# A transformer trunk on one core: the order of VectorE, GpSimd and the load queue around two changes of stage

## What is computed

```python
h = rms_norm(x, norm1_g[l])
proj = jnp.einsum('bsd,de->bse', h, w_in[l])
...
a = pool_mixer(u, pool_w[l], pool_scale[l])
b = swa_sink_attention(q, k, v, q_norm_g[l], k_norm_g[l], sinks[l])
x = x + jnp.einsum('bse,ed->bsd', jnp.concatenate([a, b], axis=-1), w_out[l])
h2 = rms_norm(x, norm2_g[l])
hid = jnp.square(jax.nn.relu(jnp.einsum('bsd,df->bsf', h2, w_up[l])))
x = x + jnp.einsum('bsf,fd->bsd', hid, w_down[l])
```

## Time and profile before

| what | value |
|---|---|
| median of 3 runs | 909.13 us (906.57 to 909.18) |
| the profiled execution's own time | 908.38 us |
| its span, first to last recorded instruction | 906.4 us |
| share of the span: PE, DVE, ACT, POOL | 98%, 60%, 47%, 30% |

### The profile page before, as it was taken

One profiled execution on the slowest core, in us unless ns is written; L12 is line 12 of the kernel. 1 busy time (PEld: TensorE's weight loads), 2 busy tenths in 40 slices (PEclk: granted clock), 3 DMA queues, 4 the chain that ended last, 5 costly groups with the idle time before them and its releaser, 6 DMA issues.

```text
span 906.4 us, 11042 instructions
## 1 busy us (share of the span) xinstructions
PE 883.8 (98%) x4137; PEld 731.9 (81%) x4137; DVE 542.3 (60%) x817; ACT 430.1 (47%) x777; POOL 270.6 (30%) x202
## 2 busy tenths in 40 slices
...
GB/s 313 49 24 24 71 24 47 209 117 116 47 46 25 73 229 128 128 152 185 166 137 128 136 190 140 176 319 391 279 198 97 166 206 93 70 184 55 181 82 81
DMA packets 65725, 124.20 MB, mean 137 GB/s; under 512 B 3580, under 2 KB 20488, under 8 KB 65672
## 3 DMA queue, kind: packets, MB, share of 16 engines
...
...
## 4 chain that ended last, share of the span: by engine, by line
PE 88%; DVE 5%; DMA 2%; issue 2%; ACT 2%; POOL 1%; SPq 0%; DVEq 0%; ACTq 0%
PE bank L1218 27%; PE bank L1219 27%; PE bank L1220 27%; PE bank L1241 2%; PE bank L1341 1%; PE bank L1353 1%; DMA d_raw<-in_w_down 1%; DVE h_buf L1041 1%; DMA s_in<-h_keep 1%; PE bank L1329 1%; POOL mem L478 1%; PE bank L1321 1%; DVE h_buf L1031 0%; DVE wgt L910 0%; DMA mem<-in_x 0%
## 5 line engine op out<-in xcount | busy, mean ns | idle before, releaser
L1218 PE MATMUL bank<-b_op,s_op 128*128 128x512 f32 x448 | 175.1, 391 | 3.8 <-DVE b_op L1052 3.8
L1219 PE MATMUL bank<-b_op,s_op 128*128 128x512 f32 x448 | 175.0, 391 | 0.0
L1220 PE MATMUL bank<-b_op,s_op 128*128 128x512 f32 x448 | 174.9, 390 | 0.0
L538 POOL TENSOR_TENSOR b_sum<-d_raw,d_raw 128x1024 f32<-128x1024 f32 x40 | 95.8, 2396 | 207.0 <-DVE b_op L1052 207.0
L1048 DVE TENSOR_TENSOR s_op<-s_in,s_op 128x1024 fp32r<-128x1024 f32 x56 | 72.1, 1288 | 136.2 <-ACT s_op L752 136.2
L752 ACT ACTIVATE s_op<-s_in 128x1024 fp32r<-128x1024 f32 x56 | 59.4, 1060 | 182.1 <-PE bank L1220 154.3
L1009 DVE TENSOR_TENSOR ring<-raw,ring 128x512 fp32r<-128x512 f32 x96 | 93.2, 984 | 85.8 <-ACT ring L700 84.2
L1218 PE MATMUL bank<-wgt,xs 128*128 128x256 f32 (+1 forms) x320 | 123.8, 387 | 2.7 <-DVE wgt L898 2.7
L1219 PE MATMUL bank<-wgt,xs 128*128 128x256 f32 (+1 forms) x320 | 118.9, 372 | 0.0
L1220 PE MATMUL bank<-wgt,xs 128*128 128x256 f32 (+1 forms) x320 | 118.5, 370 | 0.0
L1218 PE MATMUL bank<-xs,ring 128*128 128x512 f32 x256 | 101.4, 396 | 3.9 <-issue 2.7
...
## 6 DMA issues: line engine op xcount, KB each, us to landing
...
```

The source lines that it names most:

```text
L538: nc.gpsimd.tensor_tensor(out=b_sum[G % 2], in0=group_rows(qa, g), in1=group_rows(qb, g), op=op).then_inc(b_summed, 1)
L1218: nc.tensor.matmul(out_ap, lhs[HI], rhs[HI], start=first, stop=False, skip_group_check=chained)
L1219: nc.tensor.matmul(out_ap, lhs[HI], rhs[LO], start=False, stop=False, skip_group_check=chained)
L1220: return nc.tensor.matmul(out_ap, lhs[LO], rhs[HI], start=False, stop=last, skip_group_check=chained)
```

## The change

It has five parts. The order of the same instructions changes; no arithmetic is added or removed.

1. **VectorE and GpSimd at the end of stage 1.** `normed_x1(7)` stands ahead of `w_low(2..4)`. `weight_sums` is cut in two halves. For chunk 0 they stand behind the inverse roots of tiles 5 and 6, for chunk 1 behind those of tiles 6 and 7. `w_diff` gets a second buffer, and the counter `w_sum` becomes four semaphores.
2. **Products of chunks 0 and 1.** M6, M4, M5 of chunk 0, M6 of chunk 1, M3 of chunk 0, M4, M5 of chunk 1, M1 of chunk 2, M3 of chunk 1.
3. **VectorE's order in all of stage 2.** Where the product is M4, M5 or M2, `w_low(n + 5)` stands behind `add_z`, not ahead of it. At M2 of chunk 0 it stands behind `x_combine(3)` too.
4. **SyncE in chunk 15.** `load_s(3)` and `load_s(4)` stand ahead of `keep_h(15)`, and with them the last three B11 loads behind them.
5. **`w_down` by groups.** Each block comes in 8 loads of 512 KB, where it was 4 of 1 MB, each with its own semaphore; the first three of B12 together at G = 5.

```diff
-        w_diff = place("w_diff", 184, [P, KH, P], F32)
+        w_diff = [place(f"w_diff{i}", 184 + 2 * i, [P, KH, P], F32) for i in range(2)]
...
-               + [(c, m) for c in range(2) for m in ("M6", "M4", "M5", "M3")]
-               + [(c, m) for c in range(2, NCK) for m in UP])
+               + [(0, "M6"), (0, "M4"), (0, "M5"), (1, "M6"), (0, "M3"), (1, "M4"), (1, "M5"), (2, "M1"), (1, "M3")]
+               + [(c, m) for c in range(2, NCK) for m in UP if (c, m) != (2, "M1")])
...
-            def load_d(q, quarter):
+            def load_d(q, g):
                 i, k = int(q[1]) - 1, int(q[2]) - 1
-                js = slice(4 * quarter, 4 * quarter + 4)
-                sp.dma_start(d_raw[q][:, js, :], w_down_i[i][:, js, k * BANK:(k + 1) * BANK]).then_inc(d_in[q][quarter], 16)
+                js = slice(2 * g, 2 * g + 2)
+                sp.dma_start(d_raw[q][:, js, :], w_down_i[i][:, js, k * BANK:(k + 1) * BANK]).then_inc(d_in[q][g], 16)
...
                     sp.wait_ge(up_done, done_at(c, "M6"))
-                    for quarter in range(2):
-                        load_d("B11", quarter)
+                    for g in range(2):
+                        load_d("B11", g)
                     sp.wait_ge(up_done, done_at(c, "M4"))
-                    for quarter in range(2, 4):
-                        load_d("B11", quarter)
+                    for g in range(2, 5):
+                        load_d("B11", g)
+                    load_s(3)
+                    load_s(4)
+                    for g in range(5, 8):
+                        load_d("B11", g)
...
-            for G in range(3, 7 * NG):
+            for G in range(5, 7 * NG):
                 load_s(G)
-                if 3 <= G < 7:
+                if G == 5:
+                    for g in range(3):
+                        load_d("B12", g)
+                if 6 <= G < 11:
                     load_d("B12", G - 3)
...
+            def weight_sums(c, first=True, last=True):
+
+                r = raw[c % 2]
+                w11, w12, w21, w22 = (r[:, k:k + KH, f:f + P] for f in (0, P) for k in (0, KH))
+                if first:
+                    pool.wait_ge(raw_in[c % 2], 16 * (c // 2 + 1))
+                    if c >= 2:
+                        pool.wait_ge(w_lo, done_at(c - 2, "M7"))
+                    nc.gpsimd.tensor_tensor(out=w_diff[c % 2], in0=w11, in1=w21, op=ALU.subtract).then_inc(w_diff_ready, 1)
+                    pool.wait_ge(w_diff_ready, c + 1)
+                    nc.gpsimd.tensor_tensor(out=w21, in0=w21, in1=w22, op=ALU.add).then_inc(w_one_ready, 1)
+                if last:
+                    pool.wait_ge(w_one_ready, c + 1)
+                    pool.wait_ge(w_lo, done_at(c, "M1"))
+                    nc.gpsimd.tensor_tensor(out=w11, in0=w21, in1=w11, op=ALU.subtract).then_inc(w_two_ready, 1)
+                    pool.wait_ge(w_two_ready, c + 1)
+                    pool.wait_ge(w_lo, done_at(c, "M2"))
+                    nc.gpsimd.tensor_tensor(out=w12, in0=w12, in1=w11, op=ALU.subtract).then_inc(w_four_ready, 1)
...
             for T in range(NT + 2, 2 * NT):
                 inverse_rms(T)
...
+                if T == 2 * NT - 3:
+                    weight_sums(0, last=False)
+                if T == 2 * NT - 2:
+                    weight_sums(0, first=False)
+                    weight_sums(1, last=False)
+            weight_sums(1, first=False)
...
+            normed_x1(NT - 1)
             for n in range(2, 5):
                 w_low(n)
-            normed_x1(NT - 1)
...
-                if n + 5 < N_UP:
+                if m not in ("M4", "M5", "M2") and n + 5 < N_UP:
                     w_low(n + 5)
...
-                if m == UP[0] and c >= 2:
+                if c >= 2 and m == ("M7" if c == 2 else "M1"):
                     h_add(c - 1, SA, A21, A22, ALU.add, 4)
                     h_add(c - 1, SB, A21, A11, ALU.subtract, 4)
...
+                if m in ("M4", "M5", "M2") and n + 5 < N_UP:
+                    w_low(n + 5)
```

More of the change, by code:

```diff
@@ L183, in hybrid_trunk @@
         h_first_kept, h_rest_kept = sem("h_first_kept"), sem("h_rest_kept")
-        d_in = {q: [sem(f"d_in_{q}_{i}") for i in range(4)] for q in ("B11", "B12", "B22", "B21")}
+        d_in = {q: [sem(f"d_in_{q}_{i}") for i in range(8)] for q in ("B11", "B12", "B22", "B21")}
         s_in_landed = [sem(f"s_in_landed{i}") for i in range(3)]
@@ L218, in hybrid_trunk @@
         tok_done, tok_added = sem("tok_done"), sem("tok_added")
-        w_hi, w_lo, w_sum = sem("w_hi"), sem("w_lo"), sem("w_sum")
+        w_hi, w_lo = sem("w_hi"), sem("w_lo")
+        w_diff_ready, w_one_ready, w_two_ready, w_four_ready = (sem(n) for n in (
+            "w_diff_ready", "w_one_ready", "w_two_ready", "w_four_ready"))
         b12_kept, t_step, t_hi, t_lo = sem("b12_kept"), sem("t_step"), sem("t_hi"), sem("t_lo")
@@ L416, in _ @@
                     bring_x1(KH + G - 5)
-                if 10 <= G < 14:
+                if 10 <= G < 18:
                     load_d("B22", G - 10)
```

32 lines of the change are left out of this document (8 added, 24 removed).

## The result

| kernel | median, us | all executions | profiled execution (its span) |
|---|---|---|---|
| before | 908.62 | 906.57 to 909.18 (4) | 908.38 (906.4) |
| changed | 895.29 | 893.96 to 896.83 (4) | 896.83 (894.7) |

The ratio is 0.9853, 95% interval 0.9839 to 0.9867: 13.3 us faster. The forecast was 896.0, range 890.5 to 902.5.

A forecast was written before the change was run, and what follows sets the result against it. TensorE, busy 98% of the span, was taken to bound the kernel. 908.4 - 7.0 (stage 2 seam) - 5.7 (stage 3) = 895.7 us profiled; the median before lies 0.75 higher, so 896.4, stated as 896, range 890.5 to 902.5.

The forecast's parts named there:

- The walk from `x_combine(3)`: Start of stage 2: steps counted from S to the start of M3 of chunk 1, at S + 34.1 us.
- S: Start of `x_combine(3)` on VectorE, put at 283.1 us, with two of the four `w_low` ahead of it held.
- The seam: Stage 1 into stage 2: 7.0 us gained of the 12.6 us that TensorE lost up to 323.03.
- The transposes: Last transposes before stage 2: with `normed_x1(7)` first, their 3.36 us wait and the slow clock behind it go.
- The slow clock behind the wait: M3 of chunk 1: 1.7 us of slow TensorE clock behind a 2.9 us wait.
- the likeliest case: Whole kernel: the prediction's own case, 896 us with the clock's fall counted in; chance 0.50.
- `add_z` goes first: M3 of chunk 0: `add_z(0, 1)` no longer stands behind a `w_low`, so the wait and its 1.7 us of clock go.
- 2.72 us of cover: M3 of chunk 0: M6 of chunk 1 now lies between M5 and M3, giving the wait 2.72 us of cover.
- Stage 3: Start of stage 3: waits of groups 0 and 3 and the clock go, 0.8 + 3.1 + 1.75 = 5.7 us gained.
- `x_combine` was not late: Rival, M7 of chunk 0: all four `w_low` held, 2.4 us idle, clock falls, 899.3 us; chance 0.13.
- the seam's wait did not move to group 5: Rival, stage 3: early `load_s` delay what follows on SyncE, idleness moves to group 5, 902.1 us; chance 0.12.
- transfers of 0.5 MB did overlap: Denies a rival, stage 3 loads: 0.5 MB transfers don't overlap, 19 us slower, about 915 us; chance 0.04.

The follow-up runs named there:

- e8: The kernel before with part 1 alone: median 902.14 us, ratio 0.994 to the kernel before.
- e10: The kernel before with parts 1 and 4 alone, 1 MB loads kept: median 899.61 us, ratio 0.990 to the kernel before.
- e11: The changed kernel itself, measured again on another occasion: median 896.75 us, ratio 0.986 to the kernel before.
- e3: The changed kernel with `w_low(5)` moved behind `x_combine(3)` on VectorE: median 894.86 us, ratio 0.985 to the kernel before.
- e6: The changed kernel with part 5 undone (`w_down` in 1 MB loads), part 4 kept: median 896.83 us, ratio 0.987 to the kernel before.
- e7: The changed kernel with part 4 undone (`load_s(3)`, `load_s(4)` behind all of stage 2), part 5 kept: median 899.61 us, ratio 0.991 to the kernel before.
- e2: The changed kernel with M7 of chunk 2 also ahead of M3 of chunk 1: median 895.89 us, ratio 0.986 to the kernel before.
- e4: The changed kernel with the edits of e2 and e3 together: median 895.23 us, ratio 0.985 to the kernel before.
- e1: The changed kernel with part 2 undone (old order of products), all else kept: median 894.33 us, ratio 0.984 to the kernel before.
- e5: The changed kernel with part 3 undone, except that `w_low` stays behind `x_combine` at M2 of chunk 0: median 895.67 us, ratio 0.986.
- e12: e9 with part 5 undone too (`w_down` in 1 MB loads): median 893.64 us, ratio 0.983 to the kernel before.
- e9: The changed kernel with part 2 undone and `w_low(5)` behind `x_combine(3)` (e1 and e3 together): median 893.52 us, ratio 0.983 to the kernel before.

## Why the prediction was right, step by step

- **The walk from `x_combine(3)` was right to a few tenths; where it began was right by luck.** S was put at 8.9 us behind the first product of stage 2 and came at 8.8 (284.03 - 275.22), but two terms of its sum (277.2 + 2.3 + 3.6) were off by a microsecond each and cancelled. `normed_x1(7)`, taken at the 2.3 us of before, took 1.3. The two held `w_low`, taken at 1.2 each, took 3.47 together: GpSimd's two sums (280.26, 281.94) stretch the pair to that where an unheld one takes 1.29. From S on: load of the weights S + 13.8 (measured 13.84), landed S + 19.5 (19.6), store S + 28.2 (28.17), M3 of chunk 1 S + 34.1 (34.12). The idle time there was 2.61 where 2.9 was forecast, at M7 0.87 where 1.2 was. The seam gave 7.1 us against 7.0. That number alone does not show what gave it: with part 1 only, e8's profile needs the same time from the first product to the 17th, 50.13 us against 50.08. In it no clock fell behind the 2.15 us wait, while the changed kernel's profile has a fall. Where neither has one, it is 50.21 (e10) against 48.55 (e11), so parts 2 and 3 gave 1.7 us there.
- **The transposes** lost their 3.36 us wait. `normed_x1` took 1.28 us, not the 2.28 of before, with no effect: TensorE was not ready earlier. e8 shows that part 1 does this alone.
- **The slow clock behind the wait is the step that was put too firmly.** The 1.7 us stood in the sum as certain, since a 2.16 us wait had brought it. The product behind the wait took 4.43 us in one profile of the changed kernel and 2.87 in the other. Behind waits of 2.15 (e8), 2.21 (e10) and 2.74 us (e3) there was none in the profiled executions either, behind 2.55 (e6) and 3.10 (e7) there was. Behind the 2.43 us of e2 there was none, behind those of e4 there was. So the likeliest case was in truth two, near 894 and 896.6. The sum with the fall is near the second, and the median of 895.29 that it is held against is the middle between two pairs, a time that no execution took. In the profiled execution, against which the sum was made, it was 895.7 forecast and 896.83 measured; 1.0 of the 1.1 us is the later start of stage 2.
- **Part 2 was credited with what part 3 also gives.** "`add_z` goes first" and "2.72 us of cover" stood side by side as reasons for the loss of the wait before M3 of chunk 0, and the prediction did not ask what either would leave alone: 0.83 and 1.15 us (e1, e5). It saw the new wait before M3 of chunk 1 as the price of the seam. It is the price of part 2: the old order with part 3 waits 0.78 there.
- **Stage 3** gave 5.7 us, as forecast (4.8 from group 0 on, and 0.9 before it). 1.75 of it was the clock behind group 3's wait, which by e7's profile need not fall: part 4 is 3.1 us without it, and 2.9 or 4.3 by e7's median against the two of the changed kernel. Part 5's 0.92 us wait goes as forecast, and the 1.3 us for 0.5 MB less is right: behind the landing of the third `load_s`, B11's first load lands 2.67 to 2.72 us later in the five profiles with 1 MB, and 1.33 to 1.36 in the nine with 0.5 MB. What the prediction did not see is that part 3 brings another 0.8 us. Before, B11's first load was issued 7.5 us before ScalarE wanted it (582.66 to 590.17), in the changed kernel 8.3 (575.74 to 584.06), since part 3 brings chunk 14's stores forward against TensorE; with part 3 undone (e5) it is 7.5 again. With the smaller load alone (e5) ScalarE waits 0.17 us and group 0 none; with the earlier issue alone ScalarE waits 0.07 us (e6) or 0.85 (e12).
- **The rivals.** `x_combine` was not late, the seam's wait did not move to group 5 and transfers of 0.5 MB did overlap: from 586 to 620 us the DMA share is 0.93 and no product waits. B11's first four loads of 0.5 MB land 1.36 us apart in the changed kernel, which is their bytes at 388 GB/s (1.35). The fixed cost for each transfer that the Trainium skill's page "DMA: Bandwidth & Descriptors", section on the anatomy of one DMA, has is not seen between queued transfers here; no run measures it on a single one.

## What to carry to other kernels

Two edits to one wait must be priced apart: each alone, and what the second adds once the first is in. Here the interleaving added nothing to the reordering of VectorE's list, and moved the wait to a place where it was longer. Several short waits are safer for the clock than one long one. All 13 executions of e1, e9 and e12, whose profiles have no wait of 0.9 us or more in the seams, have a mean clock of 1.000, and so have the four of e5 with waits of up to 1.61 us; single ones of 2.1 to 3.1 us brought the slow clock in some profiles and not in others. That such a schedule is faster at the same total of idle time is not shown: e5 has about the changed kernel's total, and its median can't be told from it. An instruction that nobody needs soon must not stand ahead of one that everyone needs: one `w_low` behind `x_combine` was worth 1.0 us in the profile (e3), where the interleaving cost 0.8 (e1).

## What the runs showed of the chip

- **Whether the clock falls differs between executions of one kernel.** At a wait of 2.6 to 2.7 us in the changed kernel it fell in one profile (0.50, the 1.2 GHz level, until 321.9) and stayed at 1.00, 2.4 GHz, in the other. The fall cost 1.6 us (4.43 against 2.87 for the product behind the wait). The Trainium skill's page "TensorE: Matmul & The Clock Gate", Part 1, says of a kernel's start that the number of slow matmuls differs from run to run. These traces show the same there (next point), and of a wait in the middle.
- **The start of the kernel scatters by over a microsecond.** The matmuls of 512 columns follow each other in 0.43 us until about 12.4 us in the profile of before, and until 14.5 in that of after, although the granted clock's column says 1.00 in both. The first product of stage 2 stands between 274.07 and 275.60 us in the thirteen profiles of kernels with part 1. All of that scatter is made by 16.3 us: from TensorE's 31st matmul (14.77 us before, 15.81 after) to stage 2 it is 259.4 us in every profile, before's too. No run here settles why the column and the rate differ.
- **VectorE and GpSimd hold each other, and who comes first varies.** A pair of `h_add` took 1.29 or 2.38 us while GpSimd's sum beside it took 2.21 or 1.60. The Trainium skill's page "SBUF — State Buffer", section "SBUF: two separate sides", tells of a port pair that the first of the two holds for a whole instruction, and these rows agree. Which of the two was held moved the second store of chunk 14 and the `load_s` behind it by 1.1 us, and B11's load behind those by nothing (5.77 us behind the first store either way).
- **Loads of the same list land up to 0.8 us apart.** The first 0.5 MB load of B11 landed 12.9 to 13.7 us behind chunk 14's first store in nine profiles, the 1 MB one 14.2 to 15.0 in five. No run here settles why.
